# Two more block-product pairs per half and one more per chunk in a two-FFN decoder layer

## The reference

```python
def swiglu(x, wg, wu, wd):
    return (jax.nn.silu(x @ wg) * (x @ wu)) @ wd

f = swiglu(rmsnorm(h, ffn1_pre_g[l]), ffn1_wg[l], ffn1_wu[l], ffn1_wd[l])
h = h + FFN_RES_WEIGHT * rmsnorm(f, ffn1_post_g[l])
```

## Time and profile before

| | us |
|---|---|
| median of 3 runs (2082.16 to 2082.65) | 2082.45 |
| the profiled execution | 2081.73 |
| its span | 2079.9 |
| TensorE busy | 2067.6 (99%) |
| VectorE busy | 1680.6 (81%) |
| ScalarE busy | 1111.2 (53%) |

### The profile page before, as it was taken

One profiled execution on the slowest core, in us unless ns is written; L12 is line 12 of the kernel. 1 busy time (PEld: TensorE's weight loads), 2 busy tenths in 40 slices (PEclk: granted clock), 3 DMA queues, 4 the chain that ended last, 5 costly groups with the idle time before them and its releaser, 6 DMA issues.

```text
span 2079.9 us, 25938 instructions
## 1 busy us (share of the span) xinstructions
PE 2067.6 (99%) x9322; PEld 1711.2 (82%) x9322; DVE 1680.6 (81%) x2049; ACT 1111.2 (53%) x1252; POOL 27.7 (1%) x54
## 2 busy tenths in 40 slices
PE   9999999999999999999999999999999999999998
PEld 8888888888888788888788888888888888888886
DVE  6889889889887658998687555578898888889885
ACT  6555555556555454444556444465555555565453
POOL 0000000000000000100000000000000000000000
PEclk9999999999999999999999999999999999999999
DMA  8666556666666566776655666556566665656564
GB/s 287 220 200 205 192 191 202 202 201 193 203 195 215 171 185 191 207 202 179 177 175 175 187 191 209 192 174 208 187 202 201 202 202 187 209 190 208 197 202 162
DMA packets 211996, 409.51 MB, mean 197 GB/s; under 512 B 15114, under 2 KB 15378, under 8 KB 211521
## 3 DMA queue, kind: packets, MB, share of 16 engines
q1 hardware_dynamic: 209904, 401.26, 60.4%
q0 software_dynamic: 1856, 7.01, 1.4%
q10 hardware_dynamic: 144, 0.04, 0.0%
HBM read 406.14 MB, written 2.11 MB: 196 GB/s over the span
## 4 chain that ended last, share of the span: by engine, by line
PE 95%; DVE 2%; DMA 1%; issue 1%; ACT 0%; SPq 0%; POOL 0%; DVEq 0%; ACTq 0%; POOLq 0%
PE banks L1544 93%; PE banks L1594 2%; DVE wlo L957 1%; DMA raw<-in_ffn_wu_dram 1%; DVE res L1012 0%; DMA raw<-in_ffn_wg_dram 0%; DVE act_lo L1025 0%; DVE wsum L1150 0%; DVE wsum L1155 0%; ACT act_hi L532 0%; ACT whi L517 0%; DVE nat L1138 0%; POOL stat L430 0%; DVE comb L1169 0%; DVE comb L1165 0%
## 5 line engine op out<-in xcount | busy, mean ns | idle before, releaser
L517 ACT ACTIVATE whi<-raw 128x1024 fp32r<-128x1024 f32 x755 | 779.7, 1053 | 734.6 <-PE banks L1544 372.1
L957 DVE TENSOR_TENSOR wlo<-raw,whi 128x1024 fp32r<-128x1024 f32 x756 | 900.2, 1218 | 258.9 <-ACT whi L517 255.8
L1544 PE MATMUL banks<-whi,act_hi 128*128 128x512 f32 x1688 | 541.7, 395 | 0.8 <-DVE wlo L957 0.7
L1544 PE MATMUL banks<-whi,act_lo 128*128 128x512 f32 x1688 | 532.0, 389 | 0.0
L1544 PE MATMUL banks<-wlo,act_hi 128*128 128x512 f32 x1688 | 522.3, 389 | 0.1
L1544 PEld LDWEIGHTS banks<-whi,act_lo 128*128 128x128 f32 x1688 | 316.9, 188 | 66.8
L1544 PEld LDWEIGHTS banks<-wlo,act_hi 128*128 128x128 f32 x1688 | 316.7, 188 | 66.7 <-DVE wlo L957 1.0
L1544 PEld LDWEIGHTS banks<-whi,act_hi 128*128 128x128 f32 x1688 | 313.6, 188 | 67.2 <-issue 4.7
L1544 PE MATMUL banks<-whi,h_hi 128*128 128x512 f32 x560 | 179.2, 390 | 0.0
L1544 PE MATMUL banks<-whi,h_lo 128*128 128x512 f32 x560 | 179.0, 389 | 0.0
L1544 PE MATMUL banks<-wlo,h_hi 128*128 128x512 f32 x560 | 174.9, 389 | 0.0
(11 more groups left out here) (239 smaller groups left out, 2017.7 us busy)
## 6 DMA issues: line engine op xcount, KB each, us to landing
raw<-in_ffn_wg_dram SPq DMA_DIRECT2D x176, 512.0 KB, 3.7
raw<-in_ffn_wu_dram SPq DMA_DIRECT2D x176, 512.0 KB, 4.6
raw<-in_ffn_wd_dram SPq DMA_DIRECT2D x176, 512.0 KB, 4.7
raw<-in_w_in_dram SPq DMA_DIRECT2D x160, 512.0 KB, 3.6
raw<-in_w_out_dram SPq DMA_DIRECT2D x32, 512.0 KB, 3.6
raw<-in_w_pw_dram SPq DMA_DIRECT2D x16, 512.0 KB, 3.7
raw<-in_w_o_dram SPq DMA_DIRECT2D x16, 512.0 KB, 3.7
x_t<-in_x_tiles_dram SPq DMA_DIRECT2D x8, 256.0 KB, 6.7
```

Source lines behind the costliest of these rows:

```text
L517: nc.scalar.activation(whi[:, j % RING, 0:kts * width], raw[:, j % RING, 0:kts * width], ACT.Copy).then_inc(hi_ready, 1)
L957: nc.vector.tensor_tensor(wlo[:, j % RING, 0:n], raw[:, j % RING, 0:n], whi[:, j % RING, 0:n], ALU.subtract).then_inc(lo_ready, 1)
L1544: return nc.tensor.matmul(o, a, b, **kw)
```

## The change

- `SEVEN` becomes (1, 3, 5, 6): four pairs with seven products in each of the 20 summed chunks, so VectorE, ScalarE and TensorE each have one pair more of that kind, and pairs 5 and 6 follow one another.
- The order within a chunk is new. ScalarE: the copy of the transposed block moves from the chunk's end to after pair 0 of the next chunk, silu from after pair 1 to after pair 4, the two outer copies from after pair 6 to after pair 7. VectorE: `hidden` from after pair 1 to pair 6 (ahead of `wsum_lo`), `combine` from after pair 6 to after pair 7, its last two subtractions become one instruction of 1024 elements. TensorE: the transposes from after pair 6 to after pair 7.
- In the second half of the down stage pairs 5 and 7 join those with seven products. `FRONT` grows from 13 to 17 pairs, `REST` shrinks from 9 to 5. The block sums they need (`extra_sums`) are made at q = 20 and 21 of the first half; ScalarE rounds them there (`extra_hi`), VectorE takes the rest in the first two pairs of the second half.
- `gain` and `squares_of` for the first two column groups move from `FRONT` into `REST`, behind the last pair with seven products.
- Buffers of the activation sums are laid over one another.

```diff
-SEVEN = (1, 3, 5)
+SEVEN = (1, 3, 5, 6)
 DOWN_SEVEN = (9, 11, 13, 15, 17, 19)
+EXTRA = (5, 7)
+SEVEN_OF = (DOWN_SEVEN, DOWN_SEVEN + EXTRA)
+PLAIN = [q for q in range(DOWN_SLABS) if q not in SEVEN_OF[1]]
+FRONT = PLAIN[:1] + [q for two in zip(PLAIN[1:], SEVEN_OF[1]) for q in two]
```

In the ScalarE part, a summed chunk:

```diff
                     for q in range(UP_SLABS // 2):
+                        hi_at(2 * q)
                         if q in SEVEN:
+                            act.wait_ge(wsum_ready, 4 * seven + 3)
+                        hi_at(2 * q + 1)
+                        if q in SEVEN:
+                            weight_sums_hi(seven, first and f == 0 and q == SEVEN[0])
+                        if q == 0 and not first:
+                            hidden_copy(c - 2, group)
+                        if q == 4 and not first:
                             gate_silu(c - 1)
-                        if q == 6:
-                            act.wait_ge(wsum_used, seven_before(f, c, len(SEVEN)))
...
+                    act.wait_ge(wsum_used, seven_before(f, c, len(SEVEN)))
```

ScalarE, the down stage:

```diff
                     if q == DOWN_SEVEN[-1] + 1:
                         outer_copies(0)
+                    if q >= DOWN_SLABS - len(EXTRA):
+                        i = q - DOWN_SLABS + len(EXTRA)
+                        act.wait_ge(asum_ready, ASUMS * f + len(SEVEN) + len(DOWN_SEVEN) + i + 1)
+                        nc.scalar.activation(extra_hi[:, i], extra_sum[:, i], ACT.Copy).then_inc(asumhi_ready, 1)
...
                     hi_at(REST2 + k)
-                    if k == 1:
+                    if k == 2:
+                        squares_of(0, C11)
+                        squares_of(1, C12)
+                        act.wait_ge(squared, 2 * TT * BLK * f + 2 * TT)
                         outer_copies(1)
```

VectorE, the combination, a summed chunk and the down stage:

```diff
-                    nc.vector.tensor_tensor(comb[:, C12, :], comb[:, C22, :], comb[:, C12, :], ALU.subtract).then_inc(combined, 1)
-                    dve.wait_ge(combined, combined_count(f, c, 3))
-                    nc.vector.tensor_tensor(comb[:, C22, :], comb[:, C22, :], comb[:, C21, :], ALU.subtract).then_inc(combined, 1)
+                    nc.vector.tensor_tensor(comb[:, C12:C22 + 1, :], comb[:, C22:C22 + 1, :].to_broadcast([P, 2, CW]),
+                                            comb[:, C12:C11:-1, :], ALU.subtract).then_inc(combined, 2)
...
+                        if q == 6 and not first:
+                            hidden(c - 1)
                         if q in SEVEN:
                             weight_sums_lo(seven)
-                        if q == SEVEN[0] and not first:
-                            hidden(c - 1)
-                        if q == 6:
-                            combine(c, group)
+                    combine(c, group)
...
+                def extra_sums(i):
+
+                    q = EXTRA[i]
+                    link(nc.vector.tensor_tensor(extra_full[:, i], h_hi[:, SK * q:SK * q + SK, :], h_lo[:, SK * q:SK * q + SK, :],
+                                                 ALU.add))
...
                         combine(SUMMED + 1, 1)
+                    if q >= DOWN_SLABS - len(EXTRA):
+                        extra_sums(q - DOWN_SLABS + len(EXTRA))
...
+                    if i < len(EXTRA):
+                        extra_sums_lo(i)
                 for k in range(len(REST)):
                     lo_at(REST2 + k)
                     if k == 1:
+                        dve.wait_ge(wsum_used, down_seven(f, 1, len(SEVEN_OF[1])))
+                        gain(0, C11)
+                        gain(1, C12)
+                    if k == 3:
                         combine(SUMMED + 2, 0)
```

TensorE, a summed chunk:

```diff
-                    if not first:
-                        pe.wait_ge(hf_ready, UP_CHUNKS * f + c - 1)
...
+                                if j == 1 and not first:
+                                    pe.wait_ge(hf_ready, UP_CHUNKS * f + c - 1)
                                 slab(j, n0 + j + 1, 2 * group + j % 2, act_hi, act_lo, SK * q, KT - 1)
-                        if q == 6:
+                        if q == UP_SLABS // 2 - 1:
                             pe.wait_ge(combined, combined_count(f, c, 2))
                             hidden_transpose(c - 1, 1 - group, first)
```

More of the change, by code:

```diff
@@ L85 @@
 MIX, MIX_END, MIX_FREED = mix_chunks()
-SEVEN = (1, 3, 5)
+SEVEN = (1, 3, 5, 6)
 SUMMED = UP_CHUNKS - 1
 DOWN_SEVEN = (9, 11, 13, 15, 17, 19)
-PLAIN = [q for q in range(DOWN_SLABS) if q not in DOWN_SEVEN]
-FRONT = PLAIN[:1] + [q for two in zip(PLAIN[1:], DOWN_SEVEN) for q in two]
+EXTRA = (5, 7)
+SEVEN_OF = (DOWN_SEVEN, DOWN_SEVEN + EXTRA)
+PLAIN = [q for q in range(DOWN_SLABS) if q not in SEVEN_OF[1]]
+FRONT = PLAIN[:1] + [q for two in zip(PLAIN[1:], SEVEN_OF[1]) for q in two]
 REST = [q for q in PLAIN if q not in FRONT]
@@ L156, in build @@
         o_dsum = o_act + 4 * TT * 2 * CW
+        extra_hi, o_ehi = sb("extra_hi", [P, len(EXTRA), 4, P], f32r, over=o_act)
+        extra_lo, o_elo = sb("extra_lo", [P, len(EXTRA), 4, P], f32r, over=o_act + 16 * P * len(EXTRA))
+        extra_full, _ = sb("extra_full", [P, len(EXTRA), SK, SEQ], over=o_ehi)
+        extra_sum, _ = sb("extra_sum", [P, len(EXTRA), 4, P], over=o_elo)
+        assert o_elo + 16 * P * len(EXTRA) <= o_dsum
         down_hi, _ = sb("down_hi", [P, len(DOWN_SEVEN), 4, P], f32r, over=o_dsum)
@@ L646, in summed @@
                     for q in range(UP_SLABS // 2):
                         seven = seven_before(f, c, SEVEN.index(q)) if q in SEVEN else None
-                        for j in 2 * q, 2 * q + 1:
-                            if q in SEVEN and j % 2:
-                                act.wait_ge(wsum_ready, 4 * seven + 3)
-                            hi(j, base + UP_SLABS * c + j - RING + 1, base // RING + UP_SLABS // RING * c + j // RING + 1)
+                        hi_at(2 * q)
                         if q in SEVEN:
-                            act.wait_ge(wsum_ready, 4 * seven + 4)
-                            if not (first and f == 0 and q == SEVEN[0]):
-                                act.wait_ge(wsum_used, seven)
-                            nc.scalar.activation(wsum_hi[:], wsum[:], ACT.Copy).then_inc(wsumhi_ready, 1)
@@ L657, in summed @@
-                        if q == 1 and not first:
-                            gate_silu(c - 1)
-                        if q == 6:
-                            act.wait_ge(wsum_used, seven_before(f, c, len(SEVEN)))
-                            if first:
-                                act.wait_ge(acc_free[1], freed0[f][1] + 1)
-                            else:
-                                act.wait_ge(hidden_ready, SUMMED * f + c - 1)
-                            nc.scalar.activation(comb[:, C11, :], banks[:, 4 * (1 - group) + M1, :], ACT.Copy)
-                            nc.scalar.activation(comb[:, C22, :], banks[:, 4 * (1 - group) + M5, :],
-                                                 ACT.Copy).then_inc(outer_copied, 1)
@@ L670, in ffn @@
+                    if first:
+                        act.wait_ge(acc_free[1], freed0[f][1] + 1)
+                    else:
+                        act.wait_ge(hidden_ready, SUMMED * f + c - 1)
+                    nc.scalar.activation(comb[:, C11, :], banks[:, 4 * (1 - group) + M1, :], ACT.Copy)
+                    nc.scalar.activation(comb[:, C22, :], banks[:, 4 * (1 - group) + M5, :], ACT.Copy).then_inc(outer_copied, 1)
                 up0()
@@ L708, in ffn @@
                     quad(0, 2 * q, q)
+                    if q == 0:
+                        hidden_copy(SUMMED - 1, 1)
                     if q == 1:
@@ L1250, in quad @@
                 def quad(half, n, q, between=None):
[L1252 to L1253 removed]
+                    if q in SEVEN_OF[half]:
+                        seven = down_seven(f, half, SEVEN_OF[half].index(q))
                         weight_sums(seven, (down0 + n) // RING + 1, n % RING, False)
```

67 lines of the change are left out of this document (39 added, 28 removed).

## The result

The changed kernel takes **2101.62 us** (median of 4, 2100.3 to 2102.89) against 2082.3 of the kernel before on the same chip: ratio 1.0093, 95% interval 1.008 to 1.0106. Forecast were 2091.5 (2075 to 2100). Slower was right. The size was not: +19.3 us in place of +9.4, more than double, and just outside the range. Each execution ran on one core of one chip; the runs come from several chips, and each is compared with executions of the kernel before on its own chip. The profiled execution took 2100.3 us, its span is 2098.5, 18.6 longer than before.

The account below looks back on a forecast made before the run. TensorE, 99% busy, was taken to bound the kernel, VectorE having little room. -16.3 + 13.7 + 2.4 + 5.3 + 2.9 + 1.4 = +9.4 on the profiled 2081.73; with the median 0.7 higher, 2091.5 us, range 2075 to 2100.

Parts of the forecast that it names:

- -16.3 for 72 matmuls: Whole kernel: 24 more pairs with seven products remove 72 matmuls of 0.2267 us each from TensorE, 16.3 us less.
- VectorE takes the bound through waits for `wu` ahead of pairs 3 and 5: Up stage: load waits of 0.6 and 0.69 us a chunk put VectorE over TensorE's 41.69, 13.7 us given back.
- VectorE's own 41.16: Up stage: VectorE's work in one chunk, summed start to start without load waits, 41.16 us, 0.5 under TensorE's 41.69.
- The chunk's 42.45: Up stage: a chunk's time with 1.29 us of load waits, 0.76 over TensorE's own, in 18 chunks.
- ahead of the end of chunk 1, which was counted at 0: Up stage start: the fourth set of activation sums lies in plain chunk 0, and chunks c = 1 keep their gain: 0.
- Entry of the down stage, 2.4: Where up ends: later `combine_last` makes TensorE wait for slab 4 and at pair 3, 1.2 us per FFN, 2.4 in all.
- Pairs 20 and 21, 5.3: Down stage, first half's end: extra sums and `extra_hi` delay slabs 42 and 44, TensorE waits 2.65 us per FFN, 5.3 in all.
- Third pair, 2.9: Down stage, second half: VectorE without lead delivers slab 48's low part late, 1.45 us per FFN, 2.9 in all.
- End, 1.4: Down stage, `REST`: five slabs per column group in place of nine cover the closing chain, 0.7 us per FFN, 1.4 in all.
- the bounds of the two waits: Up stage: pair 3's wait bounded by 0 and 1.1 us; both pairs waiting 1.1 would give 43.36 us a chunk.
- That rival, loads landing later, 2108 us: Up stage: both pairs wait 1.1 us for loads, 30.1 us given back, 2108 us; chance 0.08.

Follow-up runs that it names:

- `extra_hi_late`: Changed kernel with ScalarE's high parts of the extra sums made after pairs 3 and 4 of the second half, VectorE's low parts one pair later: 2092.06 us.
- `unmerged`: Changed kernel with the combination's last two results made by two instructions of 512 elements, in place of one of 1024: 2112.29 us.

## Why the prediction was right and wrong

The direction and the mechanism were right: VectorE becomes the bound through its waits for `wu` loads. The step that failed is the size of VectorE's own work in a chunk.

- **-16.3 for 72 matmuls**: right; 41.69 a chunk was measured where nothing stood against it.
- **VectorE takes the bound through waits for `wu` ahead of pairs 3 and 5**: right in place and mechanism. Of the 22.5 us of such waits 11.9 lie ahead of pair 3 (0.6 a chunk, as forecast, though no full chunk had shown it) and 9.7 ahead of pair 5 (0.5 for 0.69). 1.29 us of waits were forecast; the chunk shown has 1.29, the mean is 0.96 by the profile's brackets and 1.2 start to start.
- **VectorE's own 41.16**: this is the term of the sum that failed. It measured 41.5 us start to start on average (41.57 in the chunk shown; 41.7 by the brackets). A sum start to start, from rows in which each instruction follows one that does not feed it, missed some 0.1 to 0.2 us at each place where an instruction waits for VectorE's own last result in the new order: 0.28 at pair 6's sums (0.1 counted) and 0.07 to 0.19 in the combination. With no slack each tenth is 1.8 us. The chunk's 42.45 became 42.78 on average: over 18 chunks 19.7 us given back for 13.7. A further 1.6 us went in the first FFN ahead of the end of chunk 1, which was counted at 0: 0.7 within the first 24 matmuls and 0.5 and 0.4 where TensorE waits for `wlo` at 58 and 84 us; what held VectorE there was not followed. (The kernel before had itself 0.6 over 18 x 42.37, hence the 20.6 of the table.)
- **Entry of the down stage, 2.4**: right, 2.9.
- **Pairs 20 and 21, 5.3**: the gap right (1.90 us for 1.95), its followers not as separate waits; start to start the gap is 2.07, 4.1 for both FFNs. `extra_hi_late` shows that the order of ScalarE was the cause.
- **Third pair, 2.9**: too low. TensorE reaches it 6.3 and 6.0 us later than before, counted from the stage's start, of which entry and gap are 3.5: 5.2 us for both FFNs, in these two stages largely in the form of slow matmuls.
- **End, 1.4**: about 2.1 are left for it; argued by difference only.
- **The range** ended at 2100 although the bounds of the two waits reached 43.36 a chunk. That rival, loads landing later, 2108 us, got 0.08; it is what happened when the changed kernel ran on another chip (2111.2), and yet another gave 2112.3 for `unmerged`. The landing time was taken for a property of the kernel, known from its one trace, when it goes with the chip or the time; the trace of before could not tell this, but the range should have been wider on that side.

## What to carry to other kernels

When a change takes a stage from the engine that bounds it to one whose slack it uses up, sum that engine's work start to start, add what each instruction waits for its own engine's last result, and treat a sum as near the bound as this one (41.16 for 41.69) as a loss until shown otherwise. A wait for a load is worth nothing to the engine's other work ahead of it: work moved from behind the wait into it is largely free (13.7 us gained of 16 expected), and work saved ahead of it comes back as waiting (0 us at pair 3, 18 us at pair 6 for the same cut). An engine with slack hides the chip's spread in landing times, and one without passes it on each time it waits; so a change that removes the last slack should be timed on more than one chip. Which chip an experiment ran on must then be known before two of them are compared.
